# Gated delta rule on one Trainium2 core: state products split into keys and queries, one subtraction for both directions

## The reference

```
def step(state, inp):
    q_i, k_i, u_i, w_i, a_i, g_i = inp
    v_new = u_i - einsum('bhcd,bhdv->bhcv', w_i, state)
    o = (einsum('bhcd,bhdv->bhcv', q_i * exp(g_i)[..., None], state)
         + einsum('bhce,bhev->bhcv', a_i, v_new))
    state = (state * exp(g_last)[..., None, None]
             + einsum('bhcd,bhcv->bhdv', k_i * exp(g_last[..., None] - g_i)[..., None], v_new))
    return state, o
```

## Time and profile before

| | us |
|---|---|
| median of 3 executions | 2201.34 (2197.03 to 2205.89) |
| span of the profiled execution (its own time) | 2203.0 |
| PE busy, share of the span | 2108.7, 96% |
| DVE busy | 1326.0, 60% |
| ACT busy | 927.3, 42% |
| mean granted clock of PE | 0.976 of full speed |
| data moved | 467.84 MB, 212 GB/s |

### The profile page before, as it was taken

The page is one execution under the profiler, slowest core; times in us unless marked ns, Lnnn a source line. Parts: engine busy times, 40 slices in busy tenths (PEclk is TensorE's granted clock), DMA queues, the critical chain, the costliest instruction groups (busy, mean ns, idle before and its releaser), DMA issues. The chain is left out here.

```text
span 2203.0 us, 42126 instructions
## 1 busy us (share of the span) xinstructions
PE 2108.7 (96%) x17446; PEld 1722.7 (78%) x17446; DVE 1326.0 (60%) x1539; ACT 927.3 (42%) x1295; POOL 582.2 (26%) x584
## 2 busy tenths in 40 slices
PE   7999999999999998988879999899999999999996
PEld 6888888999999997778865666777777777777774
DVE  6556412126575657844549658876666766666675
ACT  5665411001111106722246443166565665656664
POOL 0000000003578655943337222112111111111110
PEclk9999999999999999997889999999999999999998
DMA  3333522139888867868865541468887878878787
GB/s 137 101 100 100 157 93 99 68 103 256 228 232 227 209 172 241 255 183 223 232 221 181 161 151 58 192 239 292 300 315 288 318 275 313 312 280 324 281 296 281
DMA packets 261328, 467.84 MB, mean 212 GB/s; under 512 B 151792, under 2 KB 186736, under 8 KB 234032
## 3 DMA queue, kind: packets, MB, share of 16 engines
q1 hardware_dynamic: 179600, 394.05, 52.5%
q0 software_dynamic: 15296, 48.32, 7.4%
q10 hardware_dynamic: 66272, 23.21, 4.4%
HBM read 361.93 MB, written 107.49 MB: 213 GB/s over the span
## 5 line engine op out<-in xcount | busy, mean ns | idle before, releaser
L78 DVE TENSOR_TENSOR ex_w_rest<-weights,ex_w_rounded 128x2048 fp32r<-128x2048 f32 x154 | 347.2, 2288 | 118.2 <-ACT ex_w_rounded L2999 118.2
L2999 ACT CAST ex_w_rounded<-weights 128x2048 fp32r<-128x2048 f32 x154 | 287.1, 1907 | 14.2 <-PEq L48 14.1
L2894 PE MATMUL ex_s_acc<-ex_w_rounded,ex_xt 128*128 128x512 f32 x1024 | 288.1, 395 | 0.7 <-DVE ex_xt L78 0.7
L2894 PEld LDWEIGHTS ex_s_acc<-ex_w_rounded,ex_xt 128*128 128x128 f32 x1024 | 188.3, 188 | 50.2 <-issue 13.2
L2894 PE MATMUL ex_s_acc<-ex_w_rest,ex_xt 128*128 128x512 f32 x512 | 158.1, 390 | 0.0
L85 PE MATMUL ch_wide<-normed,ch_w_rounded 128*128 128x512 f32 x384 | 153.8, 400 | 1.2 <-DVE normed_rest L78 0.5
L85 PE MATMUL ch_wide<-normed_rest,ch_w_rounded 128*128 128x512 f32 x384 | 151.8, 395 | 0.0
L85 PE MATMUL ch_wide<-normed,ch_w_rest 128*128 128x512 f32 x384 | 151.7, 395 | 0.0
L2894 PE MATMUL ex_y_acc<-ex_w_rounded,ex_ht 128*128 128x512 f32 x512 | 147.6, 399 | 1.0 <-DVE ex_ht L78 1.0
L2848 POOL DMA_INDIRECT ex_xs<-hn,rt_sample_idx x16 | 21.4, 1339 | 474.0 <-PE ex_s_acc L2939 450.1
L85 PE MATMUL tk_acc<-tk_w_rounded_first,normed 128*128 128x336 f32 x400 | 127.7, 319 | 1.6 <-PEq L48 1.6
(11 more groups left out here) (426 smaller groups left out, 4654.4 us busy)
## 6 DMA issues: line engine op xcount, KB each, us to landing
weights<-in_w_expert SPq DMA_DIRECT2D x154, 1024.0 KB, 8.9
ex_weights<-in_w_expert SPq DMA_DIRECT2D x38, 1024.0 KB, 8.9
tk_w<-in_w_tok SPq DMA_DIRECT2D x10, 1344.0 KB, 7.2
ch_w<-in_w_ch SPq DMA_DIRECT2D x24, 512.0 KB, 4.4
sc_rows<-rows SPq DMA_DIRECT2D x40, 256.0 KB
sc_qk<-qkv_ch SPq DMA_DIRECT2D x40, 256.0 KB, 6.2
laq<-sc_laq ACTq DMA_DIRECT2D x80, 128.0 KB, 3.7
dl_kv<-qkv_tok SPq DMA_DIRECT2D x40, 256.0 KB, 4.0
```

What stands on the lines that cost most here:

```text
L78: return dve.tensor_tensor(out, whole, rounded.bitcast(F32), ALU.subtract)
L2894: mm = pe.matmul(banks[:, b], x[:, k, x_part], w[:, i % SPLIT, kk, 512 * b:512 * b + 512], start=(k == 0 and x_part == 0 and w is w_hi), s ...
L2999: act.copy(w_hi[:, i % SPLIT], raw(i)).then_inc(w_rounded, 1)
```

## The change

`from_state` becomes two functions. `keys_by_state` multiplies the 64 key columns of each head and direction by the state and stands where `from_state` stood; `queries_by_state` multiplies the 64 query columns and stands behind `solve`. `uobank` is laid out anew: for each parity two banks by group of four heads (`a`), each with a region for key results (index 0) and one for outputs (index 1), and in both regions the forward and the backward direction lie on different halves of the partitions. The key products are issued in `waves`, so that the two directions write to different banks at a time, as `product` does already; `to_output` takes the same order. With both directions' key results in one region, `remainder` is one subtraction over 128 partitions, and ACT's copy of the output one copy over 128 partitions. The counts of `r_out` and `o_out` follow; `kq_done` is called `keys_done` and rises after the key products. Loads and stores, POOL's work and all sizes of SBUF tiles are as before.

```diff
-        uobank = ps("dl_uobank", [P, 2, 2, NH, HD])
+        uobank = ps("dl_uobank", [P, 2, 2, 2, 4, HD])
...
-                        sp.wait_ge(kq_done, p + 1)
+                        sp.wait_ge(keys_done, p + 1)
...
-                def from_state(s, b):
+                def waves():
+
+                    return ((d, rows, (w + d) % 2, n) for w in range(2) for n in range(4) for d, rows in enumerate(halves))
+
+                def keys_by_state(s, b):
...
-                        pe.wait_ge(o_out, 2 * s - 2)
+                        pe.wait_ge(o_out, s - 1)
                     passed(s)
-                    for h in range(NH):
-                        for d, rows in enumerate(halves):
-                            mm = pe.matmul(uobank[:, b % 2, d, h, :], kq[b][rows, h, :], state[rows, h, :], start=(h == 0), stop=False, skip_group_check=True)
-                    mm.then_inc(kq_done, 1)
+                    for d, rows, a, n in waves():
+                        mm = pe.matmul(uobank[rows, b % 2, a, 0, n, :], kq[b][rows, 4 * a + n, rows], state[rows, 4 * a + n, :], start=True, stop=True, skip_group_check=True)
+                    mm.then_inc(keys_done, 1)
+
+                def queries_by_state(b):
+                    for d, rows, a, n in waves():
+                        pe.matmul(uobank[halves[1 - d], b % 2, a, 1, n, :], kq[b][rows, 4 * a + n, halves[1 - d]], state[rows, 4 * a + n, :], start=(n == 0), stop=False, skip_group_check=True)
...
-                    for h in range(NH):
-                        for d, rows in enumerate(halves):
-                            mm = pe.matmul(uobank[halves[1 - d], b % 2, d, h, :], at[b][rows, h, :], vb[rows, h, :], start=False, stop=True, skip_group_check=True)
+                    for d, rows, a, n in waves():
+                        mm = pe.matmul(uobank[halves[1 - d], b % 2, a, 1, n, :], at[b][rows, 4 * a + n, :], vb[rows, 4 * a + n, :], start=False, stop=True, skip_group_check=True)
...
-                    from_state(s, b)
+                    keys_by_state(s, b)
                     if more:
                         across(s + 1, nb, ni)
                     solve(s, b)
+                    queries_by_state(b)
                     if more:
                         correction(s + 1, nb)
                         to_state(s, b)
                     to_output(s, b)
...
-                    for d in range(2):
-                        half = slice(HD * (1 - d), HD * (1 - d) + HD)
-                        act.copy(ostage[half, b % 2], uobank[half, b % 2, d]).then_inc(o_out, 1)
-                    act.wait_ge(o_out, 2 * s + 2)
+                    act.copy(paired(ostage[:, b % 2]), uobank[:, b % 2, :, 1]).then_inc(o_out, 1)
+                    act.wait_ge(o_out, s + 1)
...
-                    for d in range(2):
-                        half = slice(HD * d, HD * d + HD)
-                        dve.tensor_tensor(r[half], rhs[half, b], uobank[half, b % 2, d], ALU.subtract).then_inc(r_out, 1)
+                    dve.tensor_tensor(paired(r[:]), paired(rhs[:, b]), uobank[:, b % 2, :, 0], ALU.subtract).then_inc(r_out, 1)
```

More of the change, by code:

```diff
@@ L1622, in phase_delta @@
         xt_ready, rhs_ready, prepared = sem("dl_xt_ready"), sem("dl_rhs_ready"), sem("dl_prepared")
-        lx_done, corrected, kq_done, v_done, kd_done, at_done = (sem(f"dl_{n}_done") for n in ("lx", "corrected", "kq", "v", "kd", "at"))
+        lx_done, corrected, keys_done, v_done, kd_done, at_done = (sem(f"dl_{n}_done") for n in ("lx", "corrected", "keys", "v", "kd", "at"))
         prod_out, xt_out, r_out, kept_out, v_out, o_out = (sem(f"dl_{n}_out") for n in ("prod", "xt", "r", "kept", "v", "o"))
@@ L1739, in solve @@
                     pe.wait_ge(xt_out, 2 * s + 2)
-                    pe.wait_ge(r_out, 2 * s + 2)
+                    pe.wait_ge(r_out, s + 1)
                     if not early(s, 1):
@@ L1782, in step @@
                     to_output(s, b)
-                idle_bank = uobank[:, 1, 0].rearrange("p h c -> p (h c)")[:, 0:P]
+                idle_bank = uobank[:, 1, 0, 0].rearrange("p h c -> p (h c)")[:, 0:P]
                 keep_busy(pe, idle_bank, ident, 4)
@@ L1835, in remainder @@
                 def remainder(s, b):
-                    dve.wait_ge(kq_done, s + 1)
+                    dve.wait_ge(keys_done, s + 1)
                     dve.wait_ge(rhs_ready, s + 1)
-                    for d in range(2):
-                        half = slice(HD * d, HD * d + HD)
-                        dve.tensor_tensor(r[half], rhs[half, b], uobank[half, b % 2, d], ALU.subtract).then_inc(r_out, 1)
+                    dve.tensor_tensor(paired(r[:]), paired(rhs[:, b]), uobank[:, b % 2, :, 0], ALU.subtract).then_inc(r_out, 1)
                 def keep(s, b):
```

## The result

The changed kernel takes 2213.42 us (median of 13 executions, 2208.29 to 2218.09), the kernel before 2205.18 on the same chip (13 executions, 2197.03 to 2209.26). The ratio is 1.0049, with a 95% interval of 1.0038 to 1.0060: slower, by 8 to 13 us, on the edge of what a measurement can tell from no change. The prediction (2180, 2166 to 2194) has the wrong sign and its range doesn't hold the time.

What follows compares the result with a forecast made beforehand. It took PE's chain from state to state, with a falling clock, as the bound, and DMA loads as the next: −20.5 us in 17 steps and −1.0 behind them, from 2201.3 to 2180 us, range 2166 to 2194.

Steps and rivals of the forecast that it cites:

- step 1: Key products alone at the head of a step: the subtraction can start sooner, −0.86 us a step.
- step 2: DVE's pair of subtractions becomes one: 0.69 instead of 1.41 us, −0.72 us a step.
- step 3: Queries behind `solve`: 1.08 us more matmuls, partly under a wait; `solve` to `to_state` 2.85 instead of 1.91, +0.94 a step.
- step 4: ACT's output copy over 128 partitions: 0.58 instead of 1.18 us, nothing on the path, perhaps −0.6 at the phase's end.
- step 7: Phase behind its first 17 steps: 12.74 us stay, the last part gains 0.6 and 0.4, together −1.0 us.
- the second stretch: Phase from the end of its first 17 steps to kernel step 18's `across`: 12.74 us, expected to stay.
- the cross-check: PE's own work in a step, five 64x64 and two 32x32 products: 6.78 of 6.94 us, so PE becomes the bound.
- Step 5: PE's clock in the first 17 steps never falls: 118.0 us, 31.0 less than 149.03.
- The second rival: PE's clock falls as before, costing 1.19 us a step: 138.2 us for 17 steps, 2189 in all; chance 0.20.
- Step 6: DMA loads pace the first 17 steps: 125 us of transfers plus 3.5 of waits, 128.5, 7.56 a step, −20.5.
- The rival on the other side: PE's clock stays low, slower than before: 10.57 us a step if all is low, +30.7, 2232 us; chance 0.06.
- the halves cost as two wholes: Key and query products each take 1.94 us as the undivided set did: 8.66 a step, 2198 us, no change; chance 0.04.

Runs made afterwards that it cites:

- e14: Changed kernel with PE's loop written out and loads of keys, queries and solve operand two heads wide from the fifth step on: 2187.92 us, ratio 0.9940 to before.
- e2: Changed kernel without the product of queries by state and that part of the output: 2187.91 us, ratio 0.9939 to the kernel before.
- e12: Kernel before with one more fp32 product of 128 rows by 448 columns a step, in the idle time before `solve`: 2193.19 us, ratio 0.9958.
- e3: Changed kernel with the query products of four of eight heads left out: 2212.22 us, ratio 1.0057 to the kernel before.
- e8: Changed kernel with `solve` as 8 products of 128x128 for both directions, POOL writing zeros beside the blocks: 2226.81 us, ratio 1.0114 to the kernel before.
- e1: Kernel before with PE's loop written out, other engines keeping theirs: 2201.79 us, ratio 1.0003.
- e4: Changed kernel with PE's loop written out: 2203.43 us, ratio 1.0005 to the kernel before.
- e9: Changed kernel with `solve` and `to_state` each as 8 products of 128x128 for both directions: 2205.35 us, ratio 1.0018 to the kernel before.
- e13: Kernel before with one more fp32 product of 128 rows by 192 columns a step, in the idle time before `solve`: 2194.44 us, ratio 0.9970.

## Why the prediction was wrong

The durations of its first four steps came out. Keys alone start the next stage 1.08 us on (step 1). The subtraction is one of 0.69 us (step 2):

```profile
980.61 0.69 DVE L1843 TENSOR_TENSOR dl_r<-dl_rhs,dl_uobank 128x512 f32<-128x512 f32 x1 [2.89 <-PE dl_uobank L1728]
```

`solve` starts 1.97 us behind the keys instead of 3.55, and with queries and `correction` it is 2.75 from `solve` to `to_state`, 2.85 expected (step 3). A step undisturbed is 6.64 us, 6.94 expected (in e14, where PE runs the same products, one from 996.86 to 1003.50 takes as long, with a wait of 0.4 in it). The copy of the output is 0.58 us (step 4), and what follows step 17 came 0.9 us shorter, 1.0 expected (step 7). Its split was partly luck: the second stretch, said to stay, gave 0.4 of it, and the last one 0.5:

```profile
1142.95 0.58 ACT L1809 COPY dl_ostage<-dl_uobank 128x512 f32<-128x512 f32 x1 [1.25 <-PE dl_uobank L1775]
```

What failed is step 3 and the cross-check behind it. It took PE's own work as the sum of its stages' durations, 6.78 us, and made PE the bound by that; step 3 charged the sixteen added matmuls with 1.08 us of work and nothing for being instructions. They are 64 more to fetch in each step, and carry the loop over what stays loaded. 17 steps at the undisturbed 6.64 would be 112.9 us, 45.3 less than the 158.2 measured. Waits at "issue" are 34.3 us, some 2 of them the regular 0.2 before `solve` that the 6.64 already hold. Most of the rest is slower products: PE is busy for 6.37 us in the step shown above, 108.3 in 17 such steps, and was busy for 121.15. Neither the sum nor a rival had such a term. The order of PE's instructions showed +16 matmuls a step, and the profile of before had "q8 instruction" with 116 packets; I read neither against the loop.

Step 5 took the clock as never low. It was low for a quarter of the stretch (0.88). That a step with keys alone at its head can keep the clock, e2 bears out (without the queries): it is 1.00 from 1042.87 to 1076.52. But an idle time alone doesn't lower it. Those five steps of e2 have waits of 0.8 to 1.2 us before `to_state`, as long as the 0.92 us of the kernel before:

```profile
1052.93 0.97 PE L1712 MATMUL dl_vsbank<-dl_v,dl_kd 64*64 64x64 f32 x26 [0.92 <-ACT dl_v L1802]
```

What e2 lacks is the product of 64x128 ahead of its waits, so the whole stretch that step 5 named (that product, short ones, then idle) fits better than the idle time by itself; no run parts them. That filling the idle time is enough, e12 shows. The second rival put 1.19 us a step on the clock; e12 gave back 1.01 of that in steps 4 to 15 (94.1 us for the twelve against 106.2).

Step 6 is in doubt as well. It let the loads set 7.56 us a step, from a share of 0.84 taken as work that can't be packed. They pack tighter: in e2 eight steps took 7.0 us each with 274 GB/s, inside step 6's 112 to 125 us for 17 (119 at that pace), and not at the upper end that it took. Whether 17 steps would have come out below its 128.5 us if instructions cost nothing, no run shows: e2, whose first turn still waits for code, took 133.4.

The rival on the other side was a clock that stays low; the clock was higher than before. That the halves cost as two wholes fell with step 1: 32 products of 64x64 take 1.08 us where 32 of 64x128 take 1.94, so the doubling that the prediction had drawn from the Trainium skill's overhead (TensorEngine Tiling (Array Packing), Instruction Overhead) isn't there. Whether an overhead is part of the 1.08 no run shows. The count of instructions did cost, in their supply.

## What to carry to other kernels

Count the instructions that a change adds to an engine's loop body as a cost of their own, and look at the instruction queue's packets in a stretch of the loop behind its first turn: none means that the loop stays loaded, and then a change that fits it has to keep it so. Waits at "issue" in the middle of a stage, between two instructions with nothing to wait for, are the sign that PE waits for its code. And where an engine's clock falls behind a short idle time that can't be removed, one wide product in it can be worth more than a shorter chain: here a gain of 0.4% for four instructions a step, against a loss of 0.5% from a change whose sum for an undisturbed step was right within 0.3 us.

## What the runs showed of the hardware

- A loop on TensorE stays loaded with 4 x 388 instructions and a few semaphore instructions (e12: 8 packets from 1000 to 1100 us, none of them from 1035 to 1080) and no longer with 4 x 416 (e3 and e8: 22 and 20 packets, 10 and 9 of them from 1035 to 1080). The limit lies between; a ring of two steps a turn was not tried.
- Where it doesn't stay, the waits at the jump back are 3.3 to 5.6 us, sometimes with a second of 2.5 to 3.2 right behind (e3, e8), and no shorter with the DMA engines at a share of 0.71 (5.34 and 5.29 us) than at 0.83 (5.15 and 3.77).
- A straight run all but hides its fetches at 384 instructions in 8.6 us (e1: no wait inside a stage over 1.0 us). With 448 instructions a step, in steps of 7 us, it doesn't: the longest wait is 3.4 us at a DMA share of 0.86 (e4) and 1.8 at 0.76 (e14).
- Sixteen records of 128x128 by 64 columns take 1.97 us, 32 of 64x64 by 64 columns 1.15 (e9): half the count of instructions, and more time.
- An fp32 product of 128x128 by 448 columns takes 1.02 us, and kept the granted clock at 1.00 where it had been 0.80 (e12, 1000 to 1100 us); with 192 columns it was 0.98 (e13).
- A wait of 0.8 to 1.2 us in each step doesn't by itself lower the granted clock: it stood at 1.00 over five such steps of e2.
